# Dummy products on TensorE, norm squares added on VectorE, and the last expert weights in four parts

## The chip, the cores and the metric

The program runs on one core of one Trainium2 chip. A core has five engines that run their own instruction streams and meet only at semaphores: TensorE (PE, with its weight loads as PEld), VectorE (DVE), ScalarE (ACT), GpSimd (POOL) and SyncE (SP), which here issues all DMA. The metric is the device time of one execution in microseconds. Three timed runs of the kernel before took 2309.2, 2311.67 and 2313.76 us.

## The reference

Everything is float32, one batch of 256 tokens, 1024 channels. Cut to its order:

```python
def first_block(x, mem, ...):                 # two layers
    mem_n = rms_norm(mem, mem_norm_g)
    for layer in range(2):
        xn = rms_norm(h, norm_mix_g[layer])   # layer 0: gla_group + rwkv7_group; layer 1: rglru + mlstm
        h = h + mixed @ w_mix_out[layer]
        h = h + memory_cross_attention(rms_norm(h, norm_xattn_g[layer]), mem_n, ...)
        h = h + conv_glu_ffn(rms_norm(h, norm_ffn_g[layer]), ...)
    return rms_norm(h, final_norm_g)

def second_block(x, c, ...):
    h = modulate(rms_norm_2(x, g_pre_mix), shift_m, scale_m)
    y = hybrid_mixer(h, ...)                  # dilated attention + hgrn2
    x = x + gate_m * rms_norm_2(y, g_post_mix)
    h = modulate(rms_norm_2(x, g_pre_ffn), shift_f, scale_f)
    y = moe_ffn(h, ...)                       # 32 experts, the best 4 for each token
    return x + gate_f * rms_norm_2(y, g_post_ffn)
```

An expert takes its tokens through w_gu (1024 to 2048), a clipped gated activation and w_down (1024 to 1024). All 32 experts' weights are read, 12 MB for each.

## The kernel before

Each engine's program is written out by hand as functions named after stage and engine (`mixer0_p` for PE, `mixer0_s` for ACT, `mixer0_v` for DVE), and each engine runs its program strictly in order. A mark is a named semaphore value; `wait_ge("name")` waits for it. The stages follow one another: in0 (first norm, small projections), gla and rwkv (first mixer), xa0, ffn0, the second mixer, xa1, ffn1, mix2 (attention and hgrn2), and moe.

**Products.** A float32 product of `P.mm` runs as two passes, so the trace shows two MATMUL for each. PSUM has eight banks of 512 columns; `P.tile(name)` takes the next main bank and waits until its last reader has freed it.

**Norms.** Activations lie with channels on partitions as 8 blocks of 128 x 256. ACT squares them in pairs into `SQ` (marks `q0` to `q3`); `sum_p` (728) multiplies each of the 8 blocks by `ONESD`, all entries 1/1024, and adds up in a bank: 8 products. `root_s` (ACT) and `root_v` (DVE) make the inverse root, and `scaled_v` scales block by block.

**Dummies.** `P.warm(name, lhsT, rhs, n)` runs n products into a fresh bank that nobody reads. Some are there already, behind `pa`, and in the router stage.

**Side work.** `P.beside(...)` registers a generator of products that are independent of the stage (keys and values of the memory, attention heads); `P.fill(name, n)` runs n steps of it, a step of kv being two products.

**Weights.** They come in 2 MB units of 16 KB a partition into slots (three in `ring`, one in `kv`, and later three in `arena` and one in place of `MIX`). SP goes through a fixed order of loads. `Feed.load` waits for the mark `used` of the slot's last unit, then for the load four before it (`FLIGHT = 4`), and issues one DMA. PE waits for `load <unit>` in `P.unit` and sets `used` behind its last product.

**Experts.** `moe_p` goes through 15 jobs; a job is one, two or four experts with 128, 64 or 32 token places each, so that a product of 512 columns runs for all of the job's experts at once on parts of the array. In each job `up_p` makes four tiles h00, h01, h10, h11 from w_gu, the activation is turned, and `contract_p` of the job before makes d0 and d1 from w_down, with `scatter_p` adding them to the output banks. The last job, q1, has four experts; behind its h11 come `contract_p` and `scatter_p`, and then the end: norm and residual on DVE and ACT, and the output DMA. In the first job, `second()` runs `biases_p` (output bias into four banks, 32 rows of weights), `sorted_p` (the experts' order, which DVE's `sorted_v` copies out and SP needs from the third job on), the turn and the next job's routing, all between h10 and h11.

The lines that set how the last unit is used:

```python
def expand_p(P, b, x, units, first, sig):
    w = [P.unit(u).rearrange("p (k n) -> p k n", k=8) for u in units]   # waits for all four
    for c in range(8):
        for g in range(len(units)):
            P.mm(b[o, :], x[:, c, o], w[g][:, c, :], first and c == 0, c == 7, ...)
```

## Time and profile before

| | |
|---|---|
| median of three timed runs | 2311.67 us |
| profiled execution | 2312.33 us |
| its span, first to last instruction | 2310.5 us |
| mean granted TensorE clock | 0.967 |
| PE busy | 2155.1 us (93%) |
| PE weight loads busy | 1426.8 us (62%) |
| DVE busy | 606.2 us (26%) |
| ACT busy | 370.4 us (16%) |
| POOL busy | 125.2 us (5%) |
| DMA moved | 587.55 MB, mean 254 GB/s |
| chain that ended last | PE 71%, DMA 25%, DVE 2% |

Busy shares are of the whole span, and the kernel has stages with different limits, so the table alone says little. PE's 93% holds stretches in which PE sets the pace and others in which it has just enough to do; the chain's 25% of DMA lies in one piece near the end. The granted clock is a share of 2.4 GHz; it has two levels, 1.00 and 0.50 (1.2 GHz).

### The profile page before, as it was taken

What the parts mean: (1) busy time and instruction counts of PE and PEld (TensorE: products, weight loads), DVE (VectorE), ACT (ScalarE), POOL (GpSimd) and SP (SyncE); (2) the same over time, 40 slices, a digit from 0 to 9 for tenths busy, and PEclk for the clock granted to TensorE, in tenths of its full rate; (3) what the DMA queues carried; (4) which work ended last, traced back from release to release, by engine and by line L of the source; (5) the groups of instructions that cost most, each with busy time, mean ns of one, the idle gap of its engine ahead of it and who ended that gap; (6) DMA issues with size and microseconds to landing.
All of it is one profiled execution on the core that took longest, in us unless ns stands there. A gap on an engine that the chain in (4) does not pass through costs nothing.

```text
span 2310.5 us, 25674 instructions
## 1 busy us (share of the span) xinstructions
PE 2155.1 (93%) x10738; PEld 1426.8 (62%) x10738; DVE 606.2 (26%) x1209; ACT 370.4 (16%) x672; POOL 125.2 (5%) x186
## 2 busy tenths in 40 slices
PE   8999999999999999999999999996779999999764
PEld 6787878888878888888777854432323333433221
DVE  3344432233444313336224331000001010100001
ACT  3421112100005212000123231110000010001000
POOL 0023300000000000000000000010000000001000
PEclk9999999999999999999999999998889999999887
DMA  6221043333541535336533449999999999999995
GB/s 247 81 102 38 2 183 128 146 146 137 232 174 46 189 139 219 146 144 264 212 149 117 171 192 381 428 426 428 427 427 415 428 426 428 426 396 428 427 428 250
DMA packets 42572, 587.55 MB, mean 254 GB/s; under 512 B 5152, under 2 KB 5424, under 8 KB 6736
## 3 DMA queue, kind: packets, MB, share of 16 engines
q1 hardware_dynamic: 42448, 585.82, 62.2%
q8 instruction: 87, 1.43, 0.3%
q14 instruction: 37, 0.30, 0.0%
HBM read 584.75 MB, written 1.05 MB: 254 GB/s over the span
## 4 chain that ended last, share of the span: by engine, by line
PE 71%; DMA 25%; DVE 2%; ACT 1%; issue 1%; SPq 0%; PEld 0%; DVEq 0%; ACTq 0%; PEldq 0%
PE pb L409 70%; DMA ring<-in_gu 8%; DMA kv<-in_gu 7%; DMA ring<-in_dne 5%; DMA kv<-in_dne 3%; PE pb L419 1%; DMA arena<-in_gu 1%; DMA arena<-in_dne 1%; ACT arena L370 1%; DVE arena L326 1%; DMA arena<-in_dn 1%; DVE arena L311 0%; DMA col<-in_cols 0%; DVE ring L326 0%; DVE arena L320 0%
## 5 line engine op out<-in xcount | busy, mean ns | idle before, releaser
L409 PE MATMUL pb<-arena,ring 128*128 128x256 f32 (+3 forms) x2688 | 600.7, 382 | 5.8 <-DVE arena L326 3.6
L409 PE MATMUL pb<-arena 128*128 128x256 f32 (+12 forms) x2772 | 525.6, 385 | 40.3 <-DMA ring<-in_dne 26.0
L409 PEld LDWEIGHTS pb<-arena,ring 128*128 128x128 f32 (+3 forms) x2688 | 503.7, 189 | 95.2 <-issue 17.1
L409 PEld LDWEIGHTS pb<-arena 128*128 128x128 f32 (+5 forms) x2772 | 344.7, 170 | 209.7 <-issue 169.6
L409 PE MATMUL pb<-arena,cst 128*64 128x512 f32 (+6 forms) x1032 | 337.2, 619 | 63.4 <-DMA kv<-in_gu 41.0
L409 PE MATMUL pb<-ring,cst 128*64 128x512 f32 (+2 forms) x800 | 342.0, 629 | 0.0
L409 PEld LDWEIGHTS pb<-arena,cst 128*64 128x64 f32 (+4 forms) x1032 | 104.5, 141 | 268.8 <-issue 266.9
L409 PE MATMUL pb<-ring,arena 128*64 128x512 f32 (+2 forms) x480 | 195.2, 634 | 5.7 <-DMA arena<-in_dne 5.7
L376 ACT ACTIVATE arena<-pb 128x512 f32<-128x512 f32 (+4 forms) x123 | 68.8, 559 | 559.4 <-PE pb L419 423.9
L409 PEld LDWEIGHTS pb<-ring,cst 128*64 128x64 f32 (+2 forms) x800 | 100.0, 140 | 67.6 <-issue 67.6
L318 DVE TENSOR_SCALAR arena<-pb 128x512 f32<-128x512 f32 x30 | 20.8, 692 | 450.2 <-PE pb L409 450.2
L370 ACT ACTIVATE arena<-arena 128x512 f32<-128x512 f32 (+5 forms) x155 | 90.2, 582 | 298.9 <-DVE arena L326 270.1
L409 PE MATMUL pb<-kv,cst 128*64 128x512 f32 (+2 forms) x288 | 135.6, 626 | 0.0
L311 DVE TENSOR_TENSOR arena<-pb,arena 128x512 f32<-128x512 f32 (+4 forms) x114 | 60.8, 533 | 248.5 <-PE pb L409 240.1
L320 DVE TENSOR_SCALAR arena<-pb 128x512 f32<-128x512 f32 x30 | 20.8, 692 | 349.1 <-PE pb L409 349.1
L409 PE MATMUL pb<-arena,kv 128*128 128x256 f32 (+1 forms) x448 | 100.9, 384 | 1.2 <-ACT arena L376 1.2
L409 PEld LDWEIGHTS pb<-ring,arena 128*64 128x64 f32 (+2 forms) x480 | 63.2, 149 | 61.4 <-issue 61.4
L409 PEld LDWEIGHTS pb<-arena,kv 128*128 128x128 f32 (+1 forms) x448 | 83.9, 189 | 16.0 <-ACT arena L376 1.6
L311 DVE TENSOR_TENSOR arena<-arena 128x512 f32<-128x512 f32 (+6 forms) x136 | 81.0, 595 | 39.5 <-ACT arena L370 29.8
L376 ACT ACTIVATE memt<-pb 128x512 f32<-128x512 f32 x36 | 21.5, 597 | 376.6 <-PE pb L409 376.4
L409 PEld LDWEIGHTS pb<-arena,xs 128*128 128x128 f32 (+2 forms) x540 | 64.2, 192 | 10.3 <-issue 8.7
L409 PE MATMUL pb<-arena,xs 128*128 128x128 f32 (+4 forms) x540 | 69.7, 293 | 0.6 <-DVE arena L320 0.5
(142 smaller groups left out, 1459.0 us busy)
## 6 DMA issues: line engine op xcount, KB each, us to landing
arena<-in_gu SPq DMA_DIRECT2D x60, 2048.0 KB, 18.3
ring<-in_gu SPq DMA_DIRECT2D x50, 2048.0 KB, 19.3
arena<-in_dne SPq DMA_DIRECT2D x36, 2048.0 KB, 19.3
ring<-in_dne SPq DMA_DIRECT2D x22, 2048.0 KB, 19.4
kv<-in_gu SPq DMA_DIRECT2D x18, 2048.0 KB, 19.4
ring<-in_up SPq DMA_DIRECT2D x13, 2048.0 KB, 7.6
ring<-in_ada SPq DMA_DIRECT2D x9, 2048.0 KB, 8.0
ring<-in_wkv SPq DMA_DIRECT2D x8, 2048.0 KB, 7.6
```

What stands on the lines that cost most here:

```text
L311: self.e.tensor_tensor(out, a, b, op).then_inc(self.sem, 1)
L318: self.e.tensor_scalar(out, a, s1, None, op0).then_inc(self.sem, 1)
L320: self.e.tensor_scalar(out, a, s1, s2, op0, op1).then_inc(self.sem, 1)
L326: self.e.scalar_tensor_tensor(out, a, s, b, op0, op1, accum_out=accum).then_inc(self.sem, 1)
L370: self.e.activation(out, a, func, bias=bias, scale=scale, accum_out=accum).then_inc(self.sem, 1)
L376: self.e.activation(out, a, ACT.Copy).then_inc(self.sem, 1)
L409: r = self.e.matmul(out, lhsT, rhs, start=start, stop=stop, skip_group_check=True)
L419: r = self.e.transpose(out, a, ident)
```

## The change

- `added_v` and `added_p` replace `sum_p` for six norms (nm, xa0, xa1, f0, f1, fin): DVE adds the four pairs of squares into one, and PE runs two products instead of eight. The root of fin moves on ACT behind its wait for the second at.q tile, PE's sum of fin behind the first at.q tile, and ACT's squares of fin behind the shift of m2.
- Dummy products: 10 before and 13 behind the first sum, 4 in rwkv pair c7, 4 behind m2's sum, 2 before hgrn's first state, three single ones inside the router's tile (into columns 256 to 512 of its bank, which nobody reads), and five behind each but the last part of the last d1.
- The front: gla's `outputs` are split; the second half moves behind the second tile of rkv.v. ACT handles rkv.v2 before it copies that half. Six steps of kv products move ahead of gla.h.
- The first job: `biases_p` moves from behind h10's products to before them, `sorted_p` behind the next job's routing, and `sorted_v` between DVE's first steps of h10 and h11.
- The last job: the four w_down units of d1 are loaded as 16 DMAs of 512 KB (two of the eight blocks of each expert at a time), and `expand_parts_p` uses them part by part.

```diff
+    def load_parts(self, names, srcs, parts):
+        n = SLOT // parts
+        taken = []
+        for name in names:
+            k, before = self.take(name)
+            self.wait_ge("used " + before)
+            taken.append(k)
+        for part in range(parts):
+            for name, src, k in zip(names, srcs, taken):
+                sem = self.sems(f"slot{k}")
+                self.counts[k] += 16
+                self.ge(self.order[-FLIGHT])
+                self.order.append((sem, self.counts[k]))
+                    self.e.dma_start(self.slots[k][:, at], src[:, at]).then_inc(sem, 16)
...
+        def added_v(V, n):
+            for b in range(1, 4):
+                V.wait_ge(f"{n}.q{b - 1}", f"{n}.q{b}")
+                V.tt(SQ[:, 0:2, :], SQ[:, 0:2, :], SQ[:, 2 * b:2 * b + 2, :], ADD)
+            V.mark(f"{n}.qs")
+        def added_p(P, n):
+            b = P.tile(n + ".ss")
+            P.wait_ge(f"{n}.qs")
+            for c in range(2):
+                P.mm(b[:, 0:256], ONESD, SQ[:, c, :], c == 0, c == 1, sig=n + ".ss" if c else None)
...
+            P.warm("in0.w0", ONESD, ONESD, 10)
             sum_p(P, "n0")
+            P.warm("in0.w1", ONESD, ONESD, 13)
...
-            sum_p(P, "nm")
+            added_p(P, "nm")
...
-            proj_p(P, "ab_r.2", "rkv.v", after_first=outputs)
+            proj_p(P, "ab_r.2", "rkv.v", after_first=lambda: outputs(0))
+            outputs(1)
             P.beside(kv_p(P, 0))
+            P.fill("rw.f0", FILLS[0])
...
-            P.fill("rw.f0", FILLS[0])
...
+                if n == "c7":
+                    P.warm("rw.w", ident, cst["tri"], 4)
...
             sum_p(P, "m2", MIX)
-            sum_p(P, "fin")
-            proj_p(P, "in2.0", "at.q", xn="m2")
+            P.warm("m2.w", ident, cst["tri"], 4)
+            proj_p(P, "in2.0", "at.q", xn="m2", after_first=lambda: added_p(P, "fin"))
...
                 decayed()
+                P.warm("hg.w", ident, cst["tri"], 2)
                 state(0)
...
+                if c in (1, 3, 5):
+                    P.mm(b[:, 256:512], ident, cst["tri"], False, False)
...
+        def expand_parts_p(P, n, x, units, parts, sig):
+            width, b = 128 // len(units), P.tile(n)
+            for part in range(parts):
+                last = part == parts - 1
+                w = [P.unit_part(u, None if last else part).rearrange("p (k n) -> p k n", k=8) for u in units]
+                for c in range(8 // parts * part, 8 // parts * (part + 1)):
+                    for g in range(len(units)):
+                        P.mm(b[o, :], x[:, c, o], w[g][:, c, :], c == 0, c == 7, ...)
+                if not last:
+                    P.warm(f"{n}.w{part}", ident, cst["tri"], 5)
...
                 if late is not None:
                     contract_p(P, late, len(GROUPS[late]))
+                else:
+                    biases_p(P)
                 up_p(P, n, q, 1, len(GROUPS[n]), sel, second)
```

## Rows read from the trace of the kernel before

**Rows 1.** The page, what DMA moved in each of 40 equal slices of the span.

```profile
GB/s 247 81 102 38 2 183 128 146 146 137 232 174 46 189 139 219 146 144 264 212 149 117 171 192 381 428 426 428 427 427 415 428 426 428 426 396 428 427 428 250
```

**Rows 2.** Stretches: length; PE, PEld, DVE, ACT, POOL busy; PE clock; DMA share; GB/s.

```profile
400.00:600.00 200.00, 200.00 (x925) 173.42 (x925) 76.27 (x169) 19.61 (x40) 0.00 (x0) 1.00 0.39 142
...
1400.00:1405.00 5.00, 5.00 (x24) 1.45 (x22) 2.08 (x3) 0.00 (x0) 0.00 (x0) 1.00 0.55 167
1405.00:1410.00 5.00, 5.00 (x28) 1.72 (x26) 0.59 (x1) 0.01 (x1) 0.00 (x0) 1.00 1.00 429
```

**Rows 3.** Timeline, 0 to 60 us: start, duration, engine, line, operation, count, idle before.

```profile
6.38 6.65 PE L409 MATMUL pb<-xs,small 128*128 128x256 f32 x16 [6.38 <-DVE small L320]
...
15.52 4.13 DVE L326 SCALAR_TENSOR_TENSOR arena<-ht,col,arena 128x256 f32<-128x256 f32 x8
...
16.67 13.83 PE L409 MATMUL pb<-arena,ring 128*128 128x256 f32 x48 [3.64 <-DVE arena L326]
20.66 2.61 ACT L370 ACTIVATE xs<-arena 128x512 f32<-128x512 f32 x4 [6.61 <-DMA arena<-in_mem]
...
30.34 3.62 PE L409 MATMUL pb<-xs,small 128*128 128x256 f32 x16
...
33.80 13.98 PE L409 MATMUL pb<-arena,ring 128*128 128x256 f32 x64
```

**Rows 4.** Timeline of gla's outputs and the tile behind; one stretch's clock.

```profile
121.67 9.95 PE L409 MATMUL pb<-arena 128*128 128x128 f32 x40
...
131.55 8.99 PE L409 MATMUL pb<-arena,ring 128*128 128x256 f32 x32
...
126.00:127.00 1.00, 1.00 (x4) 0.83 (x4) 0.08 (x1) 0.04 (x1) 0.00 (x0) 0.50 0.00 0
```

**Rows 5.** Timeline, 276 to 312 us, rwkv's last pair.

```profile
291.70 1.46 PE L409 MATMUL pb<-arena 128*64 128x512 f32 x4 [2.02 <-DVE ring L311]
292.88 3.31 PE L409 MATMUL pb<-ring,arena 128*64 128x512 f32 x8
```

**Rows 6.** Timeline, 1132 to 1172 us, the start of mix2.

```profile
1149.52 3.72 PE L409 MATMUL pb<-xs,small 128*128 128x256 f32 x16 [1.67 <-ACT xs L370]
1150.27 4.13 DVE L326 SCALAR_TENSOR_TENSOR arena<-ht,small,arena 128x256 f32<-128x256 f32 x8
...
1153.07 14.48 PE L409 MATMUL pb<-arena,ring 128*128 128x256 f32 x64
```

**Rows 7.** Timeline, 1250 to 1275 us, hgrn's first state.

```profile
1264.31 1.35 PE L409 MATMUL pb<-arena 32*128 32x128 f32 x8 [0.97 <-DVE arena L311]
...
1265.59 8.58 PE L409 MATMUL pb<-arena,kv 128*128 128x256 f32 x32
```

**Rows 8.** Timeline, 1318 to 1480 us: dummies there already, the router, the transposes.

```profile
1325.41 4.48 PE L409 MATMUL pb<-cst 128*128 128x256 f32 x20
...
1340.68 5.21 PE L409 MATMUL pb<-arena 128*128 128x32 f32 x32
...
1345.70 3.65 PE L419 MATMUL pb<-cst,arena 128*128 128x128 f32 x16
```

**Rows 9.** Timeline, the first job's biases; a stretch of 1 us behind them.

```profile
1383.37 4.51 PE L409 MATMUL pb<-arena 32*128 32x512 f32 x16
...
1388.00:1389.00 1.00, 1.00 (x7) 0.79 (x6) 0.59 (x3) 0.00 (x0) 0.29 (x1) 0.50 0.84 360
```

**Rows 10.** The chain that ended last, in order of time; one ACT row of the timeline.

```profile
2266.45 19.48 DMA ring<-in_dne
2286.07 8.58 PE pb L409 x64
...
2276.31 0.60 ACT L376 ACTIVATE memt<-pb 128x512 f32<-128x512 f32 x1 [16.12 <-PE pb L409]
```

**Rows 11.** DMA issues: destination, source, count, KB each, median us to landing.

```profile
arena<-in_lru_gw SPq DMA_DIRECT2D x1, 512.0 KB, 9.0
...
arena<-in_dn SPq DMA_DIRECT2D x1, 512.0 KB, 4.7
```

More of the change, by code:

```diff
@@ L424, in tr, with unit_part @@
             self.mark(sig)
+    def unit_part(self, name, part):
+        if name not in self.asked:
+            self.m.put("lent " + name, tuple(self.lent))
+            self.asked.append(name)
+            self.lent.append(name)
+        self.wait_ge(f"load {name}" if part is None else f"load {name} part {part}")
+        k = self.m.get("slot " + name)
+        return self.slots[0 if k is None else k]
     def used(self, name):
@@ L526, in join @@
         self.since[k] = marks
+    def load_parts(self, names, srcs, parts):
[11 more added lines that the diff above has]
+                self.order.append((sem, self.counts[k]))
+                if self.e is not None:
+                    at = slice(part * n, (part + 1) * n)
+                    self.e.dma_start(self.slots[k][:, at], src[:, at]).then_inc(sem, 16)
+                self.m.put(f"load {name}" + (f" part {part}" if part < parts - 1 else ""), (sem, self.counts[k]))
     def once(self, k, name, piece, *marks):
@@ L1061, in front_p, with outputs @@
-            proj_p(P, "ab_r.2", "rkv.v", after_first=outputs)
+            def outputs(h2):
+                b = P.tile(f"gla.o{h2}")
+                P.wait_ge("free gla.sc1", "free gla.st2")
+                for q2 in range(2):
+                    hd = q2 * 2 + h2
+                    p0, j = 64 * (hd % 2), hd // 2
+                    for i in range(2):
+                        o0 = q2 * 256 + i * 128
+                        P.mm(b[:, o0:o0 + 128], gv[:, i, hd * 128:(hd + 1) * 128], gsc[:, hd % 2, j * 2 + i, :],
+                             True, False)
+                        for c in (2 * i, 2 * i + 1):
+                            if c == 0:
+                                continue
+                            end = q2 == 1 and c == 3
+                            P.mm(b[:, q2 * 256 + c * 64:q2 * 256 + c * 64 + 64], gst[p0:p0 + 64, j, c, :],
+                                 gq[p0:p0 + 64, j, c * 64:(c + 1) * 64], False, c % 2 == 1,
+                                 sig=f"gla.o{h2}" if end else None)
@@ L1150, in front_s @@
             for h2 in range(2):
+                if h2:
+                    rkv("v", 2)
                 b = S.tile(f"gla.o{h2}")
@@ L1156, in front_s @@
                 S.mark(f"gla.sq{j}")
-            rkv("v", 2)
             S.beside(kv_s(S, 0))
@@ L2226, in ffn_v @@
             f = f"f{n}"
+            added_v(V, f)
             root_v(V, f)
@@ L2556, in mixer2_v @@
             scaled_v(V, XT, HT, CA, "m2", sig="y")
+            added_v(V, "fin")
             root_v(V, "fin", out=RB1)
@@ L2922, in up_p, with up_v @@
             P.release(f"{n}.h{k}1")
-        def up_v(V, n, k, before):
+        def up_v(V, n, k, before, between=None):
             t1, t2 = tmp[k]
@@ L2929, in up_v @@
             V.free(f"{n}.h{k}0")
+            if between is not None:
+                between(V)
             b = V.tile(f"{n}.h{k}1")
@@ L3059, in moe_v @@
                     count_of(V)
-                up_v(V, n, 1, late and f"{late}.t1")
+                up_v(V, n, 1, late and f"{late}.t1", None if at else sorted_v)
         def moe_g(G):
```

53 lines of the change are left out of this document (22 added, 31 removed).

## The prediction

> **What bounds the kernel now.** I read what DMA moves in the 40 slices first [rows 1]: 2 to 264 GB/s in the first 24, then a steady 427 or so. The busy times of two kinds of stretch say the same [rows 2]: from 400 to 600 us PE is busy for 200.00 of 200 us at the full granted clock (1.00, 2.4 GHz) with DMA at 0.39; from 1400 to 1405 us DMA is at 0.55, and from 1405 us it is at 1.00 and stays there (the 19.48 us of the last 2 MB load in [rows 10] is that rate with four loads in flight). So there are three regimes: PE sets the pace up to about 1405 us, DMA from there to the last landed weight at 2286.07 us, and a tail of 24.4 us follows. What PE saves in the first regime counts whole: the loads wait for slots that PE frees, so the point at which DMA becomes full moves with PE. What PE saves between 1405 and 2286 us counts nothing. In the tail, work behind the last landing counts whole. I add up against the profiled execution: 2312.33 us, 1.83 us more than its span; the median of the three timed runs, 2311.67 us, is 0.66 us lower, which is less than the runs differ, so I don't correct.
>
> Prices used throughout: a product of two passes over 256 columns is 2 x 13.98/64 = 0.437 us [rows 3]; eight of them against ONESD 3.62 us, so 0.45 each [rows 3]; a dummy product of 256 columns 4.48/10 = 0.45 us [rows 8].
>
> **Part by part: the start.** Now PE starts its first sum when x is squared, and 16 passes take 6.65 us, 0.416 us each, twice the 0.218 us of later ones: PE is at its lower level (1.2 GHz) [rows 3]. It then waits 3.64 us for the first scaled pair, and the 48 passes that follow take 13.83 us against 48 x 0.218 = 10.5 us [rows 3]. The ten dummies on ONESD (128 columns, 20 passes; at the lower level 0.23 us each by the last row of [rows 8], 4.6 us) can run from about 1.5 us, when ONESD is set, to about 6.1 us, while x is still on its way: no cost. PE then has worked for five to seven microseconds by the time the sum is in its middle, about what it did before the clock rose (of the 48 passes' 13.83 us, 3.3 are lost, so some 6.6 us went at the lower level). Most of the sum then runs fast; it can't end before the last square (8.2 us) plus 0.9 us = 9.1 us, and with the clock late it ends at 10.7 us; I take 9.8 us instead of 13.03. The chain sum, root, first pair (3.64 us) puts the first ab_small product at 13.4 us; the thirteen dummies (26 passes, about 3.2 us at full rate) fill 9.8 to 13.0 us, so the clock has no reason to fall. The pairs come in 4.13 us [rows 3], which adds about 0.4 us to the 10.5: the products end at 24.3 us. The sum of mem needs its squares, which end at 20.66 + 2.61 = 23.27 us [rows 3], and now three DVE additions, of which only the last (about 0.7 us, the time of other 512-column DVE work) lies behind the last square: 24.05 us, in time. Two products instead of eight: 25.2 us. ab.0 starts there instead of at 33.80: **-8.6 us** (-7.5 to -9.3). ab.0 and ab.1 come long before; ACT and DVE work behind the sum of mem moves with it.
>
> **The front (outputs in two halves, rkv.v2 before the second copy, fill before gla.h).** From 121.67 us 40 short passes take 9.95 us, and the 32 passes behind them 8.99 us instead of 32 x 0.218 = 6.99; the clock of 126 to 127 us is 0.50 [rows 4]. About half of the 40 passes are done in the first 3.3 us; the other 6.6 us would be 3.3 at full rate. The loss is 3.3 + 2.0 = 5.3 us. What PE did ahead of the fall was nothing but such short passes. With a tile of 32 long passes between the halves, and each half 3.3 us, I expect no fall in most executions, and a fall of half the length in some: **-5.0 us** (-5.3 to -1). The gla.h products wait for ACT, which now copies and squares 2.5 us behind the second half; six steps of kv products (5.1 us of work that was there before) stand ahead of them, so this wait is covered. DVE's chain to rw.be starts at the same moment as before although PE is 5.3 us ahead; the rw.b transposes, last of the stage, are where PE could meet it, with some 4 us to spare.
>
> **rwkv, four dummies in pair c7.** PE waits 2.02 us for DVE and then takes 3.31 us for 8 passes of 512 columns, 0.41 each and nearly double [rows 5]. Dummies of 4 x 0.45 = 1.8 us fit into the wait; half of 3.31 comes back: **-1.6 us** (-1.8 to +0.3, where DVE is early and the dummies are in the way).
>
> **Squares added on DVE (xa0, f0, xa1, f1).** Six products fewer each: 6 x 0.45 = 2.6 us (the 3.62 us row, [rows 3]); the sum stands behind a whole tile of 16 products, of which eight follow the last pair, 3.5 us; the last square and the last addition take 1.4 us behind that pair. Hidden, so **-10.4 us** for four (-9 to -10.8). If DVE were late its cost would be the whole 2.1 us of three additions.
>
> **mixer2: fin.** Now PE waits 1.67 us, runs the eight products of fin, and starts at.q at 1153.07 us [rows 6]. DVE scales from 1150.27 on (0.52 us a block) and ACT adds the shift after it, so without fin's squares in front of ACT the first pair is there at about 1152.5, the last at 1155.6 us. After m2's sum PE now has four dummies (to 1149.6) and then nothing to do for 2.8 us. The tile then ends at 1159.9 instead of 1160.2 us, and two products of fin follow: +0.6 us. The 2.02 us wait of [rows 5] was enough for the clock to fall, and this one is longer; I add 0.9 us: **+1.5 us** (+0.3 to +3). The saving of six products is not got here, since the old sum filled a wait. The root of fin moves behind ACT's wait for the second at.q tile, 7 us later; DVE's final scaling goes with it, before attention needs DVE.
>
> **hgrn: two dummies.** A wait of 0.97 us, then 32 passes in 8.58 instead of 6.99 us [rows 7]. The dummies (0.9 us) fill the wait: **-1.6 us**, 0 if the short passes rather than the wait are what lowers it.
>
> **Router: three dummies.** 32 short passes (5.21 us), then 16 transposes in 3.65 us [rows 8], against about 1.95 us for 16 passes of this size at full rate. The dummies add 3 x 0.45 = 1.3 us to a stretch that partly waits for ACT. If they hold the clock, about 1.7 us come back further on; if not, they cost 1.3. The short passes resemble those of [rows 4], which let it fall: **0** (-1.8 to +1.5).
>
> **First job.** biases_p, 16 passes of only 32 rows, takes 4.51 us, and behind it the clock is 0.50 [rows 9]. It is now followed by a whole expert product. The work of the job is the same, so what can be won is one fall, 1.7 us, or nothing: **-0.8 us**. The third tile's slots come 4.5 us later, but DMA idles between there and 1405 us [rows 2]. mo.order comes a few us later; SP needs it only for the third job's weights.
>
> **The tail.** Now the last load lands at 2286.07 us and only then 64 passes run, 8.58 us; d0 has left PE free at 2276.3 us [rows 10]. After: 16 loads of 512 KB, groups of four at about 2271.2, 2276.1, 2281.0 and 2286.1 us if the rate holds. A part is 16 passes, four at a time, 4 x 0.44 = 1.7 us; five dummies are 2.24 us. PE: part 0 2276.3 to 2278.0, dummies to 2280.3, part 1 to 2282.0, dummies to 2284.2, part 2 to 2285.9, dummies to 2288.2, part 3 to 2289.9 instead of 2294.65: **-4.7 us**. The last dummies delay part 3 by 2.1 us. Does the rate hold? A 512 KB load lands 4.7 us after issue at best, 9.0 us beside others [rows 11]. Four in flight are 2.10 MB per 4.7 us, 446 GB/s, above 428; per 9.0 us 233 GB/s. The 4.7 is nearer, as the 9.0 was queued behind other loads. SP issues all parts in turn with nothing else queued behind but the outputs.
>
> The Trainium skill, "DMA: Bandwidth & Descriptors", under Bandwidth, asks for at least 1 MiB per DMA to get 75% of the peak; it speaks against the parts. By it the last 8.39 MB would take 26.1 us instead of 19.6 and the sum would be about 2286 us. No row here has 512 KB loads four deep.
>
> **Sum:** -8.6 -5.0 -1.6 -10.4 +1.5 -1.6 +0 -0.8 -4.7 = -31.2; 2312.33 - 31.2 = **2281 us**.
>
> **Rivals.** (B) The clock falls all the same: the dummies and the split change nothing. For it: in [rows 9] it fell with PE fully busy. Against it: the fall of [rows 5] follows a wait. Left are the sums, 5 x 2.6 = 13.0, and the tail, less 1.5: 2296 us. (C) The parts slow the last loads to 233 GB/s: 36 us instead of 19.6, the last part at 2302.5, its end at 2304.4 instead of 2294.65, +9.8 instead of -4.7: 2295.6 us. The page's rule is the mild form of this. (D) Slower than before: the same place, with each 512 KB load taking over 13.3 us. That is the point at which four rounds (53 us) eat the 26.5 us won elsewhere; at 18 us, twice the longest row, the end is 72 us after 2266.45, some 46 us late: 2331 us. (E) The change doesn't bring the DMA regime forward (its start is set by something other than slots): only the tail counts, 2307.6 us. Against it: DMA at 0.55 just before 1405 us, while PE is busy all the time.
>
> **Chances.** My forecast with its own spread 0.80; B 0.08, C 0.06, E 0.04, D 0.02. The own spread: all small terms at their good ends 2274 us; one large term (start or front) mostly missing with the fin and router terms at their bad ends 2290 us. Range 2274 to 2290; outside lie B, C, D and E, 0.20. A measurement of this kernel can tell about 0.2% (4.6 us) from no change. Faster by more: A, B, C, 0.94; within: E, 0.04; slower: 0.02.
>
> **What would show it.** ab.0 begins near 25 us and the first sum takes under 5 us; no clock of 0.50 between 120 and 140 us; the ONESD rows shrink from 160 passes to 160 - 6 x 12 = 88; the at.q tile is preceded by an idle of about 2.8 us; DMA is full from about 1378 us; the last weight lands about 20 us after d0's last one, and the scatter follows 6 us behind. I am wrong if DMA falls below 400 GB/s in the last 20 us, if PE waits for DVE at an ONESD product, or if the full-rate regime doesn't begin earlier.

## The result and the profile after

The change makes the kernel faster, by less than forecast: 2299.37 us median of five runs (2297.31 to 2303.16) against 2313.32 us for the kernel before in the same comparison; the ratio is 0.9947, 95% interval 0.9936 to 0.9959. That is 12.3 us (9.5 to 14.8). The forecast was 2281 us with a range of 2274 to 2290 us. The profiled execution took 2297.87 us, its span 2296.1 us, 14.4 us less than the span of before, so the two traces can be compared point by point.

The page of the kernel after, PE's line of part 1 and the 40 slices of what DMA moved (to be read against [rows 1]), and stretches of the kernel after (length; busy time of PE, PEld, DVE, ACT, POOL; granted clock; DMA share; GB/s):

```profile
PE 2144.3 (93%) x10768; PEld 1418.6 (62%) x10768; DVE 618.4 (27%) x1227; ACT 370.2 (16%) x672; POOL 125.7 (5%) x186
...
GB/s 248 74 110 38 2 184 129 147 149 148 244 162 59 192 130 236 154 138 287 203 116 112 174 199 398 427 428 427 427 428 410 428 427 428 420 389 427 428 427 282
```

```profile
1385.00:1390.00 5.00, 5.00 (x24) 1.46 (x20) 0.69 (x1) 0.00 (x0) 2.49 (x5) 1.00 0.54 233
1390.00:1395.00 5.00, 5.00 (x24) 1.64 (x24) 1.38 (x2) 0.00 (x0) 0.00 (x0) 1.00 0.98 351
1395.00:1400.00 5.00, 5.00 (x26) 1.77 (x24) 0.69 (x1) 1.23 (x2) 0.00 (x0) 1.00 1.01 433
```

The three regimes are still there. DMA becomes full at about 1391 us instead of 1405 [rows 2], not at 1378 as I had put it. So the missing time was lost ahead of that point. PE's timeline shows where (start, us, engine, line, operation, out<-in, count, and in brackets the idle time before the first of them and what ended it):

```profile
6.26 3.72 PE L409 MATMUL pb<-xs,small 128*128 128x256 f32 x16 [0.85 <-ACT xs L370]
...
24.83 1.03 PE L409 MATMUL pb<-xs,small 128*128 128x256 f32 x4
34.65 16.06 PE L409 MATMUL pb<-arena,ring 128*128 128x256 f32 x64 [8.78 <-DVE arena L326]
...
1251.59 1.15 PE L409 MATMUL pb<-arena 32*128 32x128 f32 x8
1256.34 1.97 PE L419 MATMUL pb<-cst,xs 128*128 128x128 f32 x8 [3.60 <-DVE xs L311]
1258.10 8.36 PE L409 MATMUL pb<-arena,kv 128*128 128x256 f32 x32
```

The first three rows answer [rows 3]: up to the sum of mem all is as forecast (I had put its start at 24.05 to 24.3 us), and then PE stands for 8.78 us ahead of ab.0, which begins at 34.65 us, later than before. The last three answer [rows 7]: the transposes on L419 now come ahead of the 32 long passes and wait 3.60 us for DVE, a wait that the kernel before does not have there.

The ledger, as the time by which the kernel after is ahead at the same instruction of the two traces:

| place | ahead by, us | gained in the part | forecast |
|---|---|---|---|
| end of ab.0 | -2.9 | -2.9 | +8.6 |
| start of rwkv's pairs | 1.7 | 4.6 | 5.0 |
| behind pair c7 | 3.3 | 1.7 | 1.6 |
| behind xa0, ffn0, xa1, ffn1 | 13.7 | 4 x 2.6 | 10.4 |
| behind fin | 13.0 | -0.7 | -1.5 |
| behind hgrn | 8.6 | -4.4 | +1.6 |
| behind the router | 10.3 | 1.7 | 0 |
| behind the first job | 12.0 | 1.7 | 0.8 |
| start of d0 | 10.2 | -1.9 | 0 |
| end of the span | 14.4 | 4.2 | 4.7 |

Two rows are off by more than all others together: the start by 11.5 us and hgrn by 6.0 us. The row "start of d0" is no loss of the change: from the second job's first pass to the landing of d0's last load the eighteen traces of this case take 864.9 to 867.6 us, whichever the kernel (865.1 before, 866.9 after).

### The profile page after: what moved, and what is told of

Its sections match the earlier page's. It is cut to its first block, busy times and chain, and to the rows that moved or that the text cites. A ratio compares the mean times of both kernels' runs of the same rounds, so it can differ in the third digit from the quotient of the medians.

```text
span 2296.1 us, 25811 instructions
## 1 busy us (share of the span) xinstructions
PE 2144.3 (93%) x10768; PEld 1418.6 (62%) x10768; DVE 618.4 (27%) x1227; ACT 370.2 (16%) x672; POOL 125.7 (5%) x186
## 4 chain that ended last, share of the span: by engine, by line
PE 70%; DMA 25%; DVE 3%; ACT 1%; issue 0%; SPq 0%; DVEq 0%; ACTq 0%
PE pb L409 69%; DMA ring<-in_gu 8%; DMA kv<-in_gu 8%; DMA ring<-in_dne 5%; DMA kv<-in_dne 3%; PE pb L419 1%; DMA arena<-in_gu 1%; DMA arena<-in_dne 1%; DVE arena L326 1%; DMA arena<-in_dn 1%; DVE arena L311 0%; ACT arena L370 0%; DVE ring L326 0%; DMA ht<-in_x 0%; DVE arena L320 0%
## 5 line engine op out<-in xcount | busy, mean ns | idle before, releaser
L409 PE MATMUL pb<-arena,ring 128*128 128x256 f32 (+3 forms) x2688 | 599.0, 381 | 14.6 <-DVE arena L326 9.5
L409 PEld LDWEIGHTS pb<-arena,kv 128*128 128x128 f32 (+1 forms) x448 | 83.9, 189 | 15.7 <-ACT arena L376 1.6
## 6 DMA issues: line engine op xcount, KB each, us to landing
ring<-in_gu SPq DMA_DIRECT2D x50, 2048.0 KB, 19.3
```

Of the source, the lines that this page charges most:

```text
L409: r = self.e.matmul(out, lhsT, rhs, start=start, stop=stop, skip_group_check=True)
```

## The experiments

A ratio below is always to the kernel before on the same chip. The medians of that kernel lie between 2310.6 and 2313.3 us in the groups of runs, so runs of different groups are compared by ratio, or by stretches of their profiles; 0.0010 of the ratio is 2.3 us. "The version with both edits" is the run a_both.

### The two missing terms

**T1, the bank.** Each group of dummies takes a tile, and a tile takes the next PSUM bank of the rotation. At the start that is a rotation over four banks, and two of them are held by m0.b1 and m0.b2. Before, the tile behind the sum of mem got bank 6, which nobody had used; with two tiles more it gets bank 0, which is now that of m0.b2. This bank is read late: DVE does it behind its scaling of mem, at 33.42 us. **T2, the step.** In mixer2 the attention runs beside PE's main work, one step for each tile taken (pace 1). The tile of hgrn's two dummies is one tile more, so all that is left of the attention comes one tile earlier, its last transposes too.

> The kernel after, with the 23 dummies of the start put into banks 4 and 5, which nobody uses yet, so that the tiles behind them get the banks that they had before the change. Theory T1: in the kernel after, the two dummy tiles move the bank rotation by two, ab.0 gets the bank of m0.b2, and PE stands 8.78 us until DVE has read it (34.5 us). Then here ab.0 starts at about 25.9 us, its 64 passes take about 14.0 us and not 16.06, and all behind it comes 10.7 us earlier: 2288.7 us against 2299.4. Rival R1: the wait is for something else that the bank does not change (the weights of ab.0, the order on DVE): ab.0 stays at 34.65 us, 2299.4 us.

```diff
-            P.warm("in0.w0", ONESD, ONESD, 10)
+            P.warm("in0.w0", ONESD, ONESD, 10, bank=4)
...
-            P.warm("in0.w1", ONESD, ONESD, 13)
+            P.warm("in0.w1", ONESD, ONESD, 13, bank=5)
```

Measured: 2287.59 us, ratio 0.9902 (0.9888 to 0.9917), where after has 0.9947. PE's timeline of this run:

```profile
13.62 11.37 PE L409 MATMUL pb<-arena,ring 128*128 128x256 f32 x48 [0.74 <-DVE arena L326]
25.93 1.13 PE L409 MATMUL pb<-xs,small 128*128 128x256 f32 x4 [0.94 <-DVE xs L311]
26.90 13.98 PE L409 MATMUL pb<-arena,ring 128*128 128x256 f32 x64
```

ab.0 follows the sum of mem at once and takes 13.98 us, the full clock. (The sum itself came 1.1 us later than in the trace of after: it waited 0.94 us for DVE's additions, since ACT's squares of mem began at 22.21 us in this execution and not at 21.01. None of the other thirteen traces with these additions has such a wait.) T1 holds; R1 is out.

> The kernel after, with the two dummies of hgrn inside the tile of hg.s0 and not in a tile of their own. Theory T2: the tile of the dummies advances the attention by one step (pace 1), so its transposes at.y come 32 long passes too early and PE waits 3.60 us for DVE, and the clock then falls. Here the transposes stand behind the 32 passes again, without that wait: 6.0 us less than after, 2293.4 us; the kernel gains the 1.6 us that I forecast for hgrn. Rival R2: DVE is simply late because PE came there 13 us earlier, or the dummies do not hold the clock: the loss stays, 2299.4 us or at most 1 us less.

```diff
             def first_states():
                 decayed()
-                P.warm("hg.w", ident, cst["tri"], 2)
-                state(0)
+                state(0, 2)
...
             def state(c, dummies=0):
                 b = P.tile(f"hg.s{c}")
+                for _ in range(dummies):
+                    P.mm(b[:, 0:256], ident, cst["tri"], True, True)
```

Measured: 2292.55 us, ratio 0.9922 (0.9910 to 0.9934). PE's timeline:

```profile
1254.64 1.15 PE L409 MATMUL pb<-arena 32*128 32x128 f32 x8
1255.73 7.17 PE L409 MATMUL pb<-arena,kv 128*128 128x256 f32 x32
1262.74 1.04 PE L419 MATMUL pb<-cst,xs 128*128 128x128 f32 x8
```

The transposes stand behind the 32 passes again, nobody waits, and the passes take 7.17 instead of 8.36 us. T2 holds: 5.8 us of the forecast 6.0 come back.

> Both edits together. If T1 and T2 hold, and nothing later takes the gain: 2299.4 - 10.7 - 6.0 = 2282.7 us, with the point of full DMA at about 1372 us. Rival R3: the late stages of the front or the first loads of the expert stage were just in time and become a wait, so that only part of 16.7 us comes: 2286 to 2290 us.

Measured: 2282.23 us (2279.87 to 2283.82), ratio 0.9879 (0.9864 to 0.9893). The gain over the kernel after is 0.0068, 15.7 us, where T1 and T2 give 16.7; the two profiled executions are 17.0 us apart (spans of 2296.1 and 2279.1 us). R3, which left only 9.4 to 13.4 us, is out by the traces; by the totals alone, whose intervals reach some 3 us to each side, it would not be. The next two runs show the same mechanisms from the other side, in the kernel before and without a dummy.

> The kernel before, with no dummy, only the bank counter set so that the tile behind the sum of mem gets the bank of m0.b2, as it does in the kernel after. T1: ab.0 waits until DVE has read that bank, 42.6 us instead of 33.80, and some 2 us of lower clock follow: +8.8 to +10.9 us, 2322 to 2324 us. Rival R1 (the bank is not what held ab.0): 2313 us, no change.

```diff
-            P.main = [0, 1, 2, 3, 6, 7]
+            P.main, P.i = [0, 1, 2, 3, 6, 7], 2
```

Measured: 2322.1 us, ratio 1.0049 (1.0036 to 1.0061), 11.3 us slower. The row that answers the last one of [rows 3]:

```profile
41.86 15.78 PE L409 MATMUL pb<-arena,ring 128*128 128x256 f32 x64 [8.78 <-DVE arena L326]
```

The changed start of the bank counter costs 11 us here: the same 8.78 us of waiting for the same DVE line as in the kernel after, and 1.8 us of lower clock behind it.

> The kernel before, with the attention's side work advanced by one step ahead of hg.s0, and no dummy. T2: at.y's transposes come ahead of the 32 long passes and PE waits there about 3.6 us or more for DVE, beside the wait of 0.97 us that it has anyway: +3.5 to +5 us against before. Rival R2 (DVE is late only because PE came 13 us earlier): in the kernel before DVE is in time and the step costs nothing, 0 us.

```diff
                 decayed()
+                P.fill("hg.w", 1)
                 state(0)
```

Measured: 2316.47 us, ratio 1.0022 (1.0013 to 1.0031), 5.1 us slower (3.0 to 7.2). PE's timeline, to be read against [rows 7]:

```profile
1264.46 1.12 PE L409 MATMUL pb<-arena 32*128 32x128 f32 x8 [0.97 <-DVE arena L311]
1269.45 1.97 PE L419 MATMUL pb<-cst,xs 128*128 128x128 f32 x8 [3.86 <-DVE xs L311]
1271.21 9.14 PE L409 MATMUL pb<-arena,kv 128*128 128x256 f32 x32
```

So it is the step and not an earlier PE that makes DVE late; R2 is out.

### The tail

In the kernel after, the chain that ended last has the four rounds of parts (start, us, what):

```profile
2256.27 5.10 DMA ring<-in_dne
...
2261.52 6.17 DMA ring<-in_dne
...
2267.85 6.47 DMA ring<-in_dne
...
2274.47 4.92 DMA ring<-in_dne
...
2279.52 1.96 PE pb L409 x16
```

The last part lands at 2279.39 us, 23.1 us behind d0's start; whole blocks need 19.6 us [rows 10]. So the landing is 3.5 us late against the full rate, which I had assumed. Behind the landing 16 passes of 1.96 us stand in place of 64 of 8.58 us, 6.6 us less, and the rest of the kernel, from the scatter to the output, is 1.2 us shorter: 4.2 us are gained in all, near the 4.7 forecast, but by other terms. The 1.2 us are not shown to come from the parts: that rest takes 15.0 to 16.2 us in the five traces with whole blocks and 14.6 to 15.1 us in the others.

> The version with both edits, but the last four expert blocks come whole again, as before the change. From the start of d0 to the end of the span: 44.1 us as in the kernel before instead of 39.85 as in the kernel after, so 4.2 us later: 2286.4 us against 2282.2. Rival: the parts only look good because d0 starts at another time against the loads; then the stretch is 40 to 42 us here and the total within 2 us of 2282.2.

```diff
             for k in range(2):
-                if (n, k) == (JOBS[-1], 1):
+                if False:
                     expand_parts_p(P, f"{n}.d1", ats, units_of(n, "dn1", count), PARTS, f"{n}.d1")
...
-            F.load_parts(units_of(n, "dn1", len(GROUPS[n])), ...)
+            expert_loads(n, "dne", 1)
```

Measured: 2286.74 us, ratio 0.9896 (0.9880 to 0.9911); from d0's start (2241.4 us) to the end of the span (2286.2 us) 44.8 us, where the version with both edits has 40.0. The ratios differ by 0.0017, so the parts are worth about 4 us, as in the ledger. Of the 4.8 us between the two stretches 1.1 are a clock fall of this execution: its last 64 passes take 9.67 us and not 8.58 [rows 10].

> The version with both edits, with up to eight parts in flight instead of four (a second semaphore for odd parts). In the kernel after the 16 parts took 23.14 us, four in flight, where 19.64 us was the time of the same 8.39 MB whole. Theory T3: too little is in flight (2 MB, then each issue waits for a landing): here the last part lands some 19.6 us after the start of d0, and PE, with 4 x 2.1 us of work and 3 x 2.2 us of dummies behind d0, becomes the bound: the stretch from d0 to the end is 36.9 to 38.0 us, total about 2280 us. Rival R4: it is the size of the single load that costs (512 KB against 2 MB), however many are in flight: the last part lands 23 us after d0's start, total 2282 us.

```diff
-                sem = self.sems(f"slot{k}")
-                self.counts[k] += 16
-                self.ge(self.order[-FLIGHT])
-                self.order.append((sem, self.counts[k]))
+                c = f"{k}x" if part % 2 else k
+                sem = self.sems(f"slot{c}")
+                self.counts[c] = self.counts.get(c, 0) + 16
+                self.ge(self.order[-2 * FLIGHT])
+                self.order.append((sem, self.counts[c]))
```

Measured: 2281.28 us, ratio 0.9872 (0.9857 to 0.9887); from d0's start (2242.8 us) to the end 38.5 us, just outside the 36.9 to 38.0 expected. Stretches of this run, and behind them of the version with both edits, four in flight:

```profile
2245.00:2250.00 5.00, 5.00 (x44) 1.44 (x40) 0.00 (x0) 0.00 (x0) 0.00 (x0) 0.81 1.04 414
2250.00:2255.00 5.00, 5.00 (x43) 2.23 (x36) 0.00 (x0) 0.60 (x1) 0.00 (x0) 1.00 1.02 407
2255.00:2260.00 5.00, 5.00 (x31) 2.69 (x29) 0.00 (x0) 0.00 (x0) 0.00 (x0) 1.00 1.02 403
2260.00:2265.00 5.00, 5.00 (x35) 2.52 (x38) 0.00 (x0) 0.00 (x0) 0.00 (x0) 1.00 0.26 103
```

```profile
2240.00:2245.00 5.00, 5.00 (x36) 1.45 (x32) 0.00 (x0) 0.00 (x0) 0.00 (x0) 0.69 0.99 358
2245.00:2250.00 5.00, 5.00 (x49) 1.51 (x42) 0.00 (x0) 0.60 (x1) 0.00 (x0) 1.00 0.97 356
2250.00:2255.00 5.00, 5.00 (x30) 2.95 (x31) 0.00 (x0) 0.00 (x0) 0.00 (x0) 1.00 1.01 394
2255.00:2260.00 5.00, 4.21 (x27) 2.24 (x27) 0.00 (x0) 0.00 (x0) 0.00 (x0) 1.00 0.91 328
```

The last column is the one to read, up to the stretch in which the loads end: 403 to 414 GB/s with eight parts in flight, 356 to 394 with four, at nearly the same share of busy DMA engines. T3 holds for the rate: most of the loss comes from too little in flight, the rest (428 for whole blocks) from the size. But PE stays busy for the whole 5 us in which the last part lands, where with four in flight it is busy for 4.21: it has become the bound, with the dummies in its path, as T3 put it. So 1.5 us of the tail are gained (38.5 against 40.0), and the totals differ by 1.6 us by their ratios, which can't be told from none.

> The version with both edits, but in two parts of 1 MB for each block (12 dummies between them, since the gap is longer). The last landing comes 2 us earlier than with four parts (21.2 us after d0's start) by T3 as by R4, but twice as many passes stand behind it (4.1 instead of 2.1 us): within 1 us of 2282.2. If a 1 MB load runs at the full rate the landing is at 19.7 us and the total 2281 us.

```diff
-        REST_AT, COUNT_AT, PARTS = 2, 6, 4
+        REST_AT, COUNT_AT, PARTS = 2, 6, 2
...
-                    P.warm(f"{n}.w{part}", ident, cst["tri"], 5)
+                    P.warm(f"{n}.w{part}", ident, cst["tri"], 12)
```

Measured: 2281.71 us, ratio 0.9879 (0.9864 to 0.9894), the same as with four parts. The chain shows both halves of the trade:

```profile
2239.15 9.94 DMA ring<-in_dne
...
2249.24 10.65 DMA ring<-in_dne
2260.03 3.67 PE pb L409 x32
```

The landing is 20.9 us behind d0's start, 2.2 us sooner than with four parts, and 3.67 us of passes follow instead of 1.96. The rate was 418 to 419 GB/s. So the expectation of "within 1 us" held. The Trainium skill, "DMA: Bandwidth & Descriptors", section Bandwidth, asks for at least 1 MiB in one DMA to get 75% of the peak. Here 1 MB, four in flight, got 98% of 428 GB/s, and 512 KB got 83 to 92% four deep and 94 to 97% eight deep, so in this kernel the number in flight counts beside the size; the direction of the rule, which I had weighed and put aside, was right.

> The version with both edits (2282.2 us), the last four blocks in four parts, but no dummies between the parts. T4: PE then stands about 3 us ahead of each part, the clock falls, and the last part (2.1 us for 16 passes at the full rate) and perhaps the scatter behind it (3.7 us) run at the lower level: from d0's start to the end of the span 41.7 to 43.5 us instead of 40, total 2284 to 2286 us. Rival R5 (the dummies do nothing, the parts alone give the gain): 40 us, 2282 us.

```diff
-                if not last:
-                    P.warm(f"{n}.w{part}", ident, cst["tri"], 5)
```

Measured: 2283.99 us, ratio 0.9885 (0.9868 to 0.9901), 1.4 us more by the ratios, which the intervals don't separate from zero. From d0's start (2241.7 us) to the end of the span (2282.3 us) it is 40.6 us, nearer to R5's 40 than to T4's 41.7 to 43.5, though the trace shows the effect that T4 names:

```profile
2255.00:2260.00 5.00, 1.27 (x12) 0.50 (x16) 0.00 (x0) 0.00 (x0) 0.00 (x0) 0.97 1.01 363
2260.00:2265.00 5.00, 2.53 (x16) 0.45 (x12) 0.00 (x0) 0.00 (x0) 0.00 (x0) 0.50 0.52 197
...
2263.91 3.25 PE pb L409 x16
```

PE is busy for 1.27 of 5 us, the clock goes to 0.50 (1.2 GHz), and the last part takes 3.25 instead of 1.96 us. So the dummies save 1.3 us on the last part, and here the last landing came some 1 us sooner (22.1 us behind d0's start, against 23.1), which hides most of it. The rest behind the last part takes 15.1 us against 14.8, so the scatter lost next to nothing.

> The version with both edits, eight parts in flight and no dummies between the parts. With dummies (2281.3 us) PE was never idle from d0 to the end of the last part, and the 30 dummy passes, 7.3 us, stood in its path. T3: now the last landing, 19.3 us after d0's start, is the end, and 16 passes of 2.0 us follow at the full clock, 3.3 us at the lower: from d0's start to the end of the span 36.3 to 37.6 us instead of 38.5; total 2279 to 2280.5 us. Rival: the waits between the parts let the clock fall for more than the last part (scatter too, 3.7 us): 39 us and more, 2281.5 us or above.

The semaphores and the depth of eight of the run above, and no dummies. Measured: 2281.05 us, ratio 0.9871 (0.9856 to 0.9886); from d0's start (2241.3 us) to the end of the span (2278.5 us) 37.2 us, as T3 says, and the last part took 1.96 us. The last part landed 20.4 us behind d0's start, not the 19.3 expected. The tail is 2.8 us shorter than with both edits alone, the total 1.8 us by the ratios. The start of d0 lies between 2239.0 and 2242.8 us in the traces of these versions, which hold the same instructions up to the last job, so 2.8 us in the tail are less than one execution differs from another, and the total can't show them.

### The other parts

> The version with both edits, but with the 40 short passes of the gla outputs together again and the orders on ACT and of the fill as before the change. If the split holds the clock (4.6 us gained by the ledger), it is 0.50 for some microseconds behind the 40 passes, and the total is 2286.8 us. Rival: the clock falls at such places only by chance of the moment, and PE now comes there 9 us earlier: 2282.2 us, clock 1.00 all through.

```diff
-            proj_p(P, "ab_r.2", "rkv.v", after_first=lambda: outputs(0))
-            outputs(1)
+            proj_p(P, "ab_r.2", "rkv.v", after_first=outputs)
             P.beside(kv_p(P, 0))
-            P.fill("rw.f0", FILLS[0])
```

(and the fill and ACT's rkv.v2 at their old places). Measured: 2285.06 us, ratio 0.9886 (0.9870 to 0.9903), 1.6 us more by the ratios, which the intervals don't separate from zero. PE's timeline of this run, of the version with both edits, and of c_depth, whose front is the same as that of the version with both edits:

```profile
113.64 8.46 PE L409 MATMUL pb<-arena 128*128 128x128 f32 x40
122.03 9.05 PE L409 MATMUL pb<-arena,ring 128*128 128x256 f32 x32
```

```profile
114.16 3.61 PE L409 MATMUL pb<-arena 128*128 128x128 f32 x20
117.70 7.17 PE L409 MATMUL pb<-arena,ring 128*128 128x256 f32 x32
124.71 3.53 PE L409 MATMUL pb<-arena 128*128 128x128 f32 x20
```

```profile
113.64 3.78 PE L409 MATMUL pb<-arena 128*128 128x128 f32 x20
117.35 8.64 PE L409 MATMUL pb<-arena,ring 128*128 128x256 f32 x32
125.82 3.53 PE L409 MATMUL pb<-arena 128*128 128x128 f32 x20
```

Together the 40 short passes let the clock fall again, 8 us earlier in the kernel than in [rows 4], and the stretch costs 17.4 us against 14.1 us, 3.3 us instead of the 4.6 of the ledger. Split, the clock mostly holds, but not always: in the thirteen traces with the split front it fell in four (a_hgtile, e_after_router, c_depth and e_best; 8.6 to 8.9 us for the 32 passes between the halves instead of 7.17). In the five traces with the 40 passes together it fell in all, and the stretch took 17.4 to 18.9 us; split it took 14.1 us where the clock held and 15.7 to 15.8 where it fell. So the forecast holds with its own reserve: no fall in most executions, a fall of half the length in some.

> The version with both edits, with fin in mixer2 as before the change: eight products of fin between the sum of m2 and at.q, no dummies, no added squares, its root at the old place. By the ledger this part of the change costs 0.65 us (I had put +1.5): the stretch from the sum of m2 to the end of at.k is 0.6 us shorter here, the total 2281.6 us. Rival: the longer wait of 2.9 us ahead of at.q is what costs, and with the old order the clock does not fall at all: 1.5 to 2.5 us less, 2280 us.

```diff
-            P.warm("m2.w", ident, cst["tri"], 4)
-            proj_p(P, "in2.0", "at.q", xn="m2", after_first=lambda: added_p(P, "fin"))
+            sum_p(P, "fin")
+            proj_p(P, "in2.0", "at.q", xn="m2")
```

(with the squares, the root and the additions of fin as before the change). Measured: 2280.74 us, ratio 0.9872 (0.9855 to 0.9888), 1.6 us less by the ratios. In the version with both edits the passes behind the wait are slow:

```profile
1128.81 9.05 PE L409 MATMUL pb<-arena,ring 128*128 128x256 f32 x32 [2.93 <-ACT arena L370]
```

With the old order the 64 passes of at.q take 14.49 us behind a wait of 1.67 us, and from the sum of m2 to the end of at.k it is 38.0 us against 39.8. (Both are counted up to the attention's first pass.) So moving fin costs 1.8 us between these two traces; the ledger's 0.65 came from an execution in which the clock fell for a shorter time (7.92 us for the same 32 passes). Of the twelve traces with fin moved eight have 7.92 us and four 9.0, and the six with the old order all have 14.5 us for the 64 passes. So the cost is 0.6 us in most executions and 1.8 in some, inside the forecast's range of +0.3 to +3 and mostly below its +1.5. In the total the difference can't be told from none.

> The version with both edits, without the three dummies among the short passes of the router. If these hold the clock, as the ledger of the kernel after says (1.7 us gained there where I had put 0), the clock is 0.50 somewhere in the 20 us behind the router and the total is 1.7 us more, 2283.9 us. Rival: the clock stayed up because PE came there at another moment or with another stretch of work in front, and the dummies only cost: 1.3 us less, 2280.9 us.

```diff
-                if c in (1, 3, 5):
-                    P.mm(b[:, 256:512], ident, cst["tri"], False, False)
```

Measured: 2282.03 us, ratio 0.9878 (0.9861 to 0.9894), no difference. The clock held without them:

```profile
1317.27 4.17 PE L409 MATMUL pb<-arena 128*128 128x32 f32 x32
1321.27 1.95 PE L419 MATMUL pb<-cst,arena 128*128 128x128 f32 x16
```

against 5.21 and 3.65 us in [rows 8]. So the 1.7 us that the ledger shows at the router need not come from the dummies; PE is through the router 0.9 us earlier without them.

> The kernel after, without the three dummies among the router's short passes, nothing else. Theory T5 (they do nothing for the clock; that it held was a matter of what PE did before it came there): clock 1.00 behind the router as in the kernel after, PE 1.0 us earlier at the gather of the first job, total 2298.4 to 2299.4 us. Rival R6 (at this moment they do hold it): the 32 short passes take 5.2 us or the transposes 3.6 us again, total 2301 us.

The same edit in the kernel after. Measured: 2300.89 us, ratio 0.9952 (0.9938 to 0.9965) against 0.9947. Here the clock did fall:

```profile
1334.70 4.56 PE L409 MATMUL pb<-arena 128*128 128x32 f32 x32
1339.07 3.23 PE L419 MATMUL pb<-cst,arena 128*128 128x128 f32 x16
```

Neither expectation is right as it stands. T5 is wrong for this execution, R6 for the one above. The traces of the other runs settle the balance. Take the stretch from the last twelve dummy passes ahead of the router (1337.95 us in the trace of before) to the ten passes of 32 columns behind the transposes (1351.07 us there). In the eleven traces with the three dummies it takes 11.3 us every time. In the seven without them it takes 10.4 us three times (the clock held: d_router, b_added, e_best), 11.5 us three times (b_rotate, b_step, e_after_router) and 13.1 us once (the kernel before). Their mean is 11.3 us too: the dummies make this stretch steady and gain nothing.

> The kernel before, with the squares of xa0, f0, xa1 and f1 added on DVE, nothing else. The four sums are 2.6 us shorter each and nothing waits for DVE: 2312.3 - 10.4 = 2301.9 us, ratio 0.9955. Rival (part of it is eaten by later waits or by clock falls at other moments): 2304 to 2307 us.

```diff
-            proj_p(P, f"wq{n}.0", x + ".q0", xn=x, after_first=lambda: sum_p(P, x))
+            proj_p(P, f"wq{n}.0", x + ".q0", xn=x, after_first=lambda: added_p(P, x))
...
-                        sum_p(P, f)
+                        added_p(P, f)
```

(and added_v ahead of root_v in xattn_v and ffn_v). Measured: 2299.1 us, ratio 0.9946 (0.9932 to 0.9959): 12.5 us less (9.5 to 15.7). This one part gives as much as the whole change did. 10.4 lies in the interval. The trace shows what may have been added to it in this execution, with no dummy ahead of these passes:

```profile
289.79 1.08 PE L409 MATMUL pb<-arena 128*64 128x512 f32 x4 [2.02 <-DVE ring L311]
290.67 1.94 PE L409 MATMUL pb<-ring,arena 128*64 128x512 f32 x8
...
1253.06 7.17 PE L409 MATMUL pb<-arena,kv 128*128 128x256 f32 x32
...
1326.72 4.16 PE L409 MATMUL pb<-arena 128*128 128x32 f32 x32
1330.72 1.95 PE L419 MATMUL pb<-cst,arena 128*128 128x128 f32 x16
```

Against [rows 5], [rows 7] and [rows 8]: 1.94 us instead of 3.31, 7.17 instead of 8.58, 4.16 and 1.95 instead of 5.21 and 3.65. The first pair of rows matters most. Up to there the kernel holds the same instructions as the kernel before, with the same 2.02 us wait, and the clock did not fall.

> What held, together: both edits, fin as before the change (1.5 us less), no dummies in the router (1 us less on PE, nothing measurable in the total so far), eight parts in flight without dummies. 2282.2 - 1.5 - 0.5 - 2.5 = about 2277.7 us if the terms add; 2280 us if the tail gives nothing.

Its edit is the sum of those of the runs that it names. Measured: 2281.85 us (2276.96 to 2282.26), ratio 0.9870 (0.9855 to 0.9885). The profiled execution was the one of 2276.96 us; the other three lie at 2282. The sum of the terms, 2277.7 us, is not what the median shows, and no version from 0.9870 to 0.9879 can be told from another. Nothing here speaks for more than the plain pair of edits.

## Why the prediction was right in direction and wrong in size

- **What bounds the kernel: right.** Three regimes, and what PE saves ahead of full DMA counts whole: the two edits together moved the end by 15.7 us (0.0068 of 2312), and by 17.0 us between the two traces, where T1 and T2 put 16.7.
- **The start: the step that failed** (11.5 us) is "ab.0 starts there instead of at 33.80", together with "ACT and DVE work behind the sum of mem moves with it". The first sum in 3.72 us, the products from 13.62 us, and the sum of mem at 24.83 us came as worked out. I priced the dummies by what they put on PE ("no cost") and not by the tile that each group takes. The sentence on ACT and DVE was true and hid the point: DVE's work did move with it, but DVE reads m0.b2 only at 33.42 us, 7.6 us behind the end of the sum of mem, and with the bank moved that reader stands in front of ab.0. Before, no one had to wait for it. Shown by removing it (10.4 us back) and by making it alone (11.3 us slower).
- **hgrn: the other step that failed** (6.0 us) is "The dummies (0.9 us) fill the wait: -1.6 us". They do fill the wait, but their tile is also a step of the attention; +4.4 instead of -1.6. Shown in both directions: 5.8 us back, and 5.1 us slower. With both edits in place the ratio is 0.9879, 2284.3 us of the 2312.33 that the forecast starts from, against 2281: the other misses come to some 3 us. That the dummies hold the clock here is likely and not proved: inside the tile they stand in eleven traces, all with 7.17 us for the 32 passes, but b_added has 7.17 without them.
- **Squares on DVE: right in mechanism and size** (2.6 us at each of four places in the trace of after; 12.5 us, 9.5 to 15.7, alone). The sum of mem waited for DVE after all, by 0.94 us in one trace of fourteen; that was one of my signs of being wrong, and it weighs little.
- **The front: right** in mechanism; 4.6 us in the ledger, 3.3 us by the trace without it, and 1.6 us less than either in the four traces of thirteen in which the clock fell in spite of the split.
- **rwkv's dummies: likely, not tested alone.** The 1.7 us of the ledger equal the forecast. Of the four traces without them three show the fall (3.31 to 3.42 us for the 8 passes) and one, b_added, does not (1.94); the fourteen with them never do, and PE's wait there is 0.3 instead of 2.0 us, so they cost next to nothing.
- **fin: right in mechanism**, the idle of 2.94 us ahead of at.q and the clock fall behind it; +0.6 us in eight traces and +1.8 in four (forecast +1.5, range +0.3 to +3).
- **Router: right at 0 on the average.** The ledger's -1.7 is inside the range of my 0, but it comes from the trace of before, the slowest of seven there; over all traces the dummies gain nothing.
- **First job**: 1.7 us gained by the ledger against 0.8. Not tested alone, but every trace has the one order or the other. From the passes that open the first job's h00 (1360.35 us before, 1350.28 after) to those of the next job it takes 38.9 us in twelve of the fourteen traces with the new order and 40.5 in two, in which the clock fell behind the biases all the same (8.5 us for 32 passes instead of 7.09); with the old order 40.9 us once, in the kernel before, and 42.5 three times. So the term was put too low: some 2 to 3.6 us.
- **The tail: right in sum, wrong in terms.** "16 loads ... if the rate holds": it did not, 23.1 us instead of 19.6. In the forecast PE and its last dummies made up the end (3.8 us behind the last landing); in fact the landing was late enough that PE was never behind (2.1 us). The test named beforehand, DMA below 400 GB/s, came true, and the cause is the bytes in flight more than the size. The scatter followed 2.8 us behind the last landing, not 6.
- **"What PE saves between 1405 and 2286 us counts nothing": right as far as the traces tell.** The trace of after is 1.9 us longer there, 1.6 of them where the clock fell while PE's work and the loads alternate. But the same stretch takes 864.9 us in the trace of the version with both edits and 867.5 in that of c_whole, which do the same work up to there, so the 1.9 us are within what single executions differ by.

```profile
1915.00:1920.00 5.00, 3.80 (x11) 1.30 (x13) 0.00 (x0) 0.00 (x0) 0.00 (x0) 0.66 0.99 423
```

- **The rivals.** None of them was what happened. B put the smaller gain down to the clock and gives 2296 us, near the result by accident: the clock was only the smaller part of both losses (2.1 us of 10.9 at ab.0; 2.1 of 5.7 at hgrn). The rival that was missing is that a dummy's tile moves resources that other work counts on.

The wrong terms make up the difference: 31.2 forecast, less 11.5 and 6.0, less 0.4 and 0.5 for the front and the tail, less 1.9 in the third regime (the spread of executions), plus 1.7 for the router, 0.9 for the first job, 0.8 for fin and 0.1 for rwkv, gives the 14.4 of the two spans.

## What to carry to other kernels

Where a helper takes a buffer from a rotation or counts steps, an edit that costs nothing on its engine can still shift every later assignment: list what the call takes (bank, slot, step, semaphore) and, for the next taker, ask who must have read that buffer first. Put warm-up work into a tile that is taken anyway, or into one that nobody uses. And price a clock fall that one trace shows as something that comes in some executions: before paying a sure microsecond for dummies, measure the same stretch in several traces and compare the means.

## What the runs showed of the hardware

- The fall of the granted clock is not a property of the place alone. The same instructions up to the rwkv pair, with the same wait of 2.02 us, took 3.31, 3.42 and 3.35 us in three executions and 1.94 us in a fourth; the 32 short passes of the router took 4.16 to 5.21 us in the seven kernels without dummies there, the transposes behind them 1.94 to 3.65. Executions of one kernel go with this: in the version with hgrn's dummies inside the tile, the six runs with a mean clock of 0.972 to 0.975 took 2297.07 down to 2289.85 us.
- The clock fell with PE busy all the time, in the profile, where the work was short: in all five traces with 40 passes of at most 128 columns in a row (17.4 to 18.9 us for a stretch that takes 14.1 where the clock holds), and in four of thirteen with 20 such passes at a time (15.7 to 15.8 us).
- Loads of 512 KB, four in flight, moved 352 to 394 GB/s in full stretches of 5 us (kernel after and version with both edits) while the DMA engines were shown as busy for 0.95 to 1.02 of the time; eight in flight moved 403 to 414 at 1.02 to 1.04, 1 MB four in flight 418 to 419 at 1.01 to 1.02, and 2 MB four in flight 428. The busy share does not show the difference; the GB/s do.
- The Trainium skill, "Perfetto Trace Analysis", section Matmul Optimizations, says to use all eight PSUM banks. The start of this kernel rotates over four while banks 4 and 5 are free; giving those two to the dummies was worth 10.4 us (0.0045 of 2312), which agrees. But the number of banks was not the cause: the kernel before used no more of them there and did not wait. What counted is that ab.0 does not get a bank whose last reader is late.
